# Norm factors behind the products, and a new order of the steps around the first expert gather

## The reference, cut to what matters

```python
def rmsnorm_2(x, w):                       # one factor per token, one gain per column
    y = xf * lax.rsqrt(jnp.mean(xf * xf, axis=-1, keepdims=True) + NORM_EPS)
    return (y * w.astype(jnp.float32)).astype(x.dtype)

x = x + hybrid_mixer(...)                                  # ends in mixed @ w_out
# memory_cross_attention(h = rmsnorm_2(x, norm_xa_w), ...)
q = h @ wq
scores = einsum('bshd,bmhd->bhsm', q, k) * XA_HEAD_DIM ** -0.5
p = softmax(scores);  o = einsum('bhsm,bmhd->bshd', p, v);  x = x + o @ wo
# peer_ffn(h = rmsnorm_2(x, norm_ffn_w), ...)
q = (h @ wq).reshape(t, 8, 2, 128)
sc = einsum('thpd,hpnd->thpn', q, sub_keys)                # 2 x 128 keys per head
# top 16 of each half, top 16 of their 256 sums -> 16 experts per token and head, a softmax as gate
act = gelu(u_table[expert] . h);  out = sum(gate * act * v_table[expert])
```

## Time and profile before

| | |
|---|---|
| median of three runs | 1705.7 us |
| the profiled execution | 1705.75 us, its span 1704.5 us |
| busy share of the span | PE 89%, DVE 63%, ACT 41%, POOL 21% |
| gathers by the software queue q0 | 39.4% of the 16 DMA engines' span, 277.05 MB |
| chain that ended last | PE 59%, DMA 20%, DVE 11%, ACT 5% |

### The profile page before, as it was taken

How to read it: one execution, slowest core, us unless ns; L and a number is a source line. 1 busy time by engine, 2 the same in 40 slices (tenths; PEclk the granted TensorE clock), 3 DMA queues, 4 the chain that set the end, 5 groups by cost and what they waited for, 6 DMA issues and landing times.

```text
span 1704.5 us, 21573 instructions
## 1 busy us (share of the span) xinstructions
PE 1520.0 (89%) x7972; PEld 1130.4 (66%) x7972; DVE 1073.1 (63%) x1942; ACT 701.3 (41%) x1538; POOL 349.6 (21%) x325
## 2 busy tenths in 40 slices
PE   3999989998989999798999999988888888788786
PEld 3899988888889998798998676544433443334222
DVE  6666665776555555677665128677667677677754
ACT  2434444443444444544342114444444444444443
POOL 1100010000010000101100003444444444444451
PEclk8999999899999999888999999999999999999999
DMA  9777666656455554232333438999999999999996
GB/s 359 277 240 249 236 207 222 209 199 210 173 182 185 186 185 149 87 124 87 97 112 128 177 101 342 419 420 421 420 421 420 421 421 421 421 421 422 421 419 256
DMA packets 90858, 463.14 MB, mean 272 GB/s; under 512 B 10753, under 2 KB 10913, under 8 KB 57729
## 3 DMA queue, kind: packets, MB, share of 16 engines
q0 software_dynamic: 39216, 277.05, 39.4%
q1 hardware_dynamic: 50688, 183.52, 31.9%
q10 hardware_dynamic: 848, 1.18, 0.2%
HBM read 459.62 MB, written 2.10 MB: 271 GB/s over the span
## 4 chain that ended last, share of the span: by engine, by line
PE 59%; DMA 20%; DVE 11%; ACT 5%; issue 3%; POOL 1%; SPq 0%; DVEq 0%; ACTq 0%; POOLq 0%
DMA Ft<-peer_uv,ids 14%; PE ps L1224 8%; PE ps L464 7%; PE ps L465 7%; PE ps L466 7%; DMA uhi<-peer_uv,ids 4%; PE ps L1056 3%; DVE Ft L1973 2%; PE ps L580 2%; PE ps L581 2%; PE ps L582 2%; DMA mlo<-peer_uv,ids 2%; PE ps L1139 2%; DVE wlo L1249 2%; PE ps L508 2%
## 5 line engine op out<-in xcount | busy, mean ns | idle before, releaser
L1224 PE MATMUL ps<-Ft 128*128 128x512 f32 x796 | 384.6, 621 | 76.9 <-ACT Ft L2486 76.0
L1224 PEld LDWEIGHTS ps<-Ft 128*128 128x128 f32 x796 | 146.7, 195 | 295.6 <-ACT Ft L2486 157.7
L1973 DVE CUSTOM_DVE_ANT_0 Ft<-Ft 128x1024 f32<-128x1024 f32 x199 | 243.8, 1225 | 152.3 <-DMA Ft<-peer_uv,ids 145.2
L464 PE MATMUL ps<-uhi,whi 128*128 128x256 f32 x1088 | 315.7, 290 | 7.1 <-DVE ulo L1337 6.1
L1249 DVE TENSOR_TENSOR wlo<-raw,whi 128x1024 fp32r<-128x1024 f32 x228 | 277.7, 1244 | 70.0 <-ACT whi L1997 69.6
L465 PE MATMUL ps<-ulo,whi 128*128 128x256 f32 x1088 | 311.8, 287 | 0.0
L466 PE MATMUL ps<-uhi,wlo 128*128 128x256 f32 x1088 | 311.6, 286 | 0.0
L2612 POOL DMA_INDIRECT Ft<-peer_uv,ids x199 | 220.2, 1107 | 295.3 <-PE ps L1224 258.1
L1997 ACT ACTIVATE whi<-raw 128x1024 fp32r<-128x1024 f32 x228 | 229.6, 1048 | 27.3 <-DMA raw<-ff_gu 15.6
L464 PEld LDWEIGHTS ps<-uhi,whi 128*128 128x128 f32 x1088 | 213.4, 196 | 11.2 <-issue 8.9
L465 PEld LDWEIGHTS ps<-ulo,whi 128*128 128x128 f32 x1088 | 213.0, 196 | 2.0 <-issue 0.5
(11 more groups left out here) (419 smaller groups left out, 2269.3 us busy)
## 6 DMA issues: line engine op xcount, KB each, us to landing
raw<-ff_gu SPq DMA_DIRECT2D x88, 512.0 KB, 4.8
raw<-w_ada SPq DMA_DIRECT2D x72, 512.0 KB, 5.1
raw<-ff_dn SPq DMA_DIRECT2D x44, 512.0 KB, 4.3
raw<-w_in SPq DMA_DIRECT2D x32, 512.0 KB, 3.6
raw<-w_in_s SPq DMA_DIRECT2D x28, 512.0 KB, 4.3
raw<-w_out SPq DMA_DIRECT2D x14, 512.0 KB, 4.3
raw<-w_in_m SPq DMA_DIRECT2D x12, 512.0 KB, 4.4
raw<-xa_wk SPq DMA_DIRECT2D x8, 512.0 KB, 3.6
```

The source lines that it names most:

```text
L464: t.matmul(o, hi[:, c], x[0][:, i], start=(k == 0), stop=False)
L1224: ins = t.matmul(acc[r][c], diag[n % NDIAG], gbuf[n % NGAT][:, 1024 + c * 512:1024 + (c + 1) * 512], start=False, stop=(n % 128 == 127))
L1973: v.tensor_tensor_reduce(pjunk, gbuf[n % NGAT][:, 0:1024], xn[:, q // 8, :], 1.0, 0.0, ALU.mult, ALU.add, dots[:, n:n + 1]).then_inc(*up(" ...
```

## The change

Three things are changed together.

First, the two norms of this part (cross attention's and the experts') no longer scale before the product. `columns` transposes the raw residual half by half as soon as that half is there; the gain is applied on the copy out as before. The factor per token comes later: for cross attention in the exp (its `scale` operand, and the maximum times the factor as bias), for the experts on the copy of the key scores (`choice_k`) and in `xn`. The step `row_identity` and the diagonal products go.

Second, the order on all engines. Row 0's steps come as early as their data allow. Ahead of the first expert head's keys now stand the last of the mixer's row 1, and behind them the query of head 1, row 1's transposes and all of row 1's queries, half of which stood ahead before. Row 1's softmax is cut into three steps: "soft" 0 ahead of pair 0, "soft" 1 behind pair 0, "soft" 2 behind pair 1; `values` for the two groups stand behind pairs 2 and 3.

Third, places in memory. The weight tiles get 20 places instead of 17, of which two (17 and 18) lie under the gather buffer at 12224. That buffer moves from slot 0 to slot 3, so that `first_use` is now {3: q, 5: s, 6: pT, 7: o}, all of row 1; slot 4 follows in order. GpSimd's power for row 1's first norm moves from ahead of gather 0 to behind gather 2.

```diff
-        def norm_cols(name, r):
-            t.wait_ge(*at("ms", name, r, "dgr"))
-            for b in range(2):
-                o = bank((name, "tr", r, b))
-                for k in range(4):
-                    c = (4 * b + k) * 128
-                    ins = t.matmul(o[:, k * 128:(k + 1) * 128], h[:, r, c:c + 128], dgr[:, r, :], start=True,
-                                   stop=True)
-                ins.then_inc(*up("tr", name, r, b))
-                give((name, "tr", r, b), "xTv" if b else "xTa", name, r)
+        def columns(name, src, r, b):
+
+            o = bank((name, "tr", r, b))
+            t.wait_ge(*at("res", src, b, r))
+            for k in range(4):
+                c = (4 * b + k) * 128
+                ins = t.transpose(o[:, k * 128:(k + 1) * 128], h[:, r, c:c + 128], ident)
+            ins.then_inc(*up("tr", name, r, b))
+            give((name, "tr", r, b), *taken(name, r, b))
...
             stage(0)
-            run(rows32("mixed", T_OUT, sT, ("stage_a",), 0))
+            o = rows32("mixed", T_OUT, sT, ("stage_a",), 0)
+            run(o, 6)
+            columns("xa", "mixed", 0, 0)
+            run(o, 2)
             stage(1)
             o = rows32("mixed", T_OUT, sT, ("stage_a",), 1)
-            run(o, 2)
-            norm_cols("xa", 0)
+            run(o, 1)
+            columns("xa", "mixed", 0, 1)
             run(o, 1)
             q = queries(0)
             run(q, 6)
@@ -1174,22 +1190,29 @@
             run(q, 2)
             run(o, 1)
             scores(0, 1)
-            run(o, 2)
             values_t(0, 0)
-            run(o, 2)
+            run(o, 1)
+            values(0, 0)
+            run(o, 1)
             values_t(0, 1)
-            values(0, 0)
+            w = rows32("xa", T_XO, oT, ("oTc",), 0)
+            run(w, 1)
             values(0, 1)
-            norm_cols("xa", 1)
-            run(rows32("xa", T_XO, oT, ("oTc",), 0))
+            run(w, 5)
+            columns("ffn", "xa", 0, 0)
+            run(w, 2)
+            run(o, 1)
+            columns("ffn", "xa", 0, 1)
+            run(o, 1)
+            peer_tile(0)
+            run(o, 1)
+            peer_keys(0)
+            peer_tile(1)
+            columns("xa", "mixed", 1, 0)
+            columns("xa", "mixed", 1, 1)
+            peer_keys(1)
             q = queries(1)
-            run(q, 2)
-            norm_cols("ffn", 0)
-            run(q, 1)
-            peer_tile(0)
-            run(q, 1)
-            peer_keys(0)
-            run(q, 2)
+            run(q, 6)
...
-                if what == "soft":
+                if what == "soft" and args[0] == 2:
                     for g in range(2):
                         values_t(1, g)
-                    for g in range(2):
-                        values(1, g)
+                elif what == "val":
+                    values(1, *args)
                 elif what == "out1":
                     run(out1, 1)
                 elif what == "cols1":
-                    norm_cols("ffn", 1)
+                    for b in range(2):
+                        columns("ffn", "xa", 1, b)
                 elif what == "tile":
                     peer_tile(*args)
...
-    for q in range(1, 16):
-        p = {2: 1, 3: 13, 8: 64}.get(q, 16 * q - 40)
-        first, each = {1: (0, 1), 2: (16, 1), 3: (29, 1)}.get(q, (16 * q - 24, 2))
+    for q in range(2, 16):
+        p = {2: 4, 3: 13, 8: 64}.get(q, 16 * q - 40)
+        first, each = {2: (19, 1), 3: (29, 1)}.get(q, (16 * q - 24, 2))
         for k in range(6):
             put(first + each * k, "route", q)
         put(first + 6 * each + (5 if each == 1 else 4), "drain", q)
-        if q > 1:
-            put(p, "tile", q)
-            put(p + 4, "pq", q)
...
+    for place, *what in ((0, "soft", 1), (1, "soft", 2), (2, "val", 0), (3, "val", 1), (4, "route", 1), (5, "route", 1),
+                         (6, "turn", 0), (6, "turn", 1), (10, "drain", 1), (39, "cols1"), (43, "cols1a"), (43, "mean1"),
+                         (49, "cols1v"), (100, "rows", 1), (137, "last", 0, 0), (145, "last", 0, 1),
+                         (160, "last", 0, 2)):
+        put(place, *what)
     for k in range(8):
-        put(3 + 3 * k, "out1", k)
+        put(7 + 3 * k, "out1", k)
     for n in range(2):
-        put(22 + 12 * n, "res1", n)
-        put(23 + 12 * n, "sq1", n)
-    for place, what in ((40, "mean1"), (52, "dgr1"), (53, "cols1"), (57, "cols1a"), (62, "cols1v")):
-        put(place, what)
...
-        def row_identity(name, r):
-            v.wait_ge(*at("rs", name, r))
-            v.tensor_scalar(dgr[:, r, :], ident, stat[name][:, 6 + r:7 + r], None, ALU.mult).then_inc(
-                *up("ms", name, r, "dgr"))
...
+            if g == 0:
+                v.wait_ge(*at("rs", "xa", r))
+            v.tensor_scalar(xsm[:, c:c + 2], xsm[:, c:c + 2], stat["xa"][:, 6 + r:7 + r], -1.0, ALU.mult,
+                            ALU.mult).then_inc(*up("xa_v", "m", r, g))
...
-                                   bias=xsm[:, c + e:c + e + 1], scale=1.0 / 16.0,
+                                   bias=xsm[:, c + e:c + e + 1], scale=stat["xa"][:, 6 + r:7 + r],
                                    accum_out=xsm[:, 8 + c + e:9 + c + e])
...
-            a.activation(keyed[q], spot["pk", q][:, 0:256], ACT.Copy).then_inc(*up("peer_a", "scs", q))
+            if q % 8 == 0:
+                a.wait_ge(*at("rs", "ffn", q // 8))
+            a.activation(keyed[q], spot["pk", q][:, 0:256], ACT.Copy, scale=stat["ffn"][:, 6 + q // 8:7 + q // 8]).then_inc(
+                *up("peer_a", "scs", q))
...
-        row_power("xa", 1)
         row_power("ffn", 0)
-        first_use = {4: ("q", 1, 1), 5: ("s", 1, 1), 6: ("pT", 1, 1), 7: ("o", 1, 1)}
+        first_use = {3: ("q", 1, 1), 5: ("s", 1, 1), 6: ("pT", 1, 1), 7: ("o", 1, 1)}
...
+            if n == 2:
+                row_power("xa", 1)
+            elif n == 54:
                 row_power("ffn", 1)
-            elif n == 70:
...
+    place = list(range(13)) + [18, 17, 15, 14, 16, 13, 0, 1, 2, 3, 4, 19, 5, 6, 7, 8, 9, 10, 11, 12, 13, 0, 1, 2, 3, 4, 14]
```

More of the change, by code:

```diff
@@ L192, in peer_order @@
         put(first + 6 * each + (5 if each == 1 else 4), "drain", q)
-        if q > 1:
-            put(p, "tile", q)
-            put(p + 4, "pq", q)
[L196 to L199, removed]
+        put(p, "tile", q)
+        put(p + 4, "pq", q)
+        put(p + 6, "keys", q)
+        put(p + 10, "scs", q)
+    for place, *what in ((0, "soft", 1), (1, "soft", 2), (2, "val", 0), (3, "val", 1), (4, "route", 1), (5, "route", 1),
[3 more added lines that the diff above has]
+        put(place, *what)
     for k in range(8):
-        put(3 + 3 * k, "out1", k)
+        put(7 + 3 * k, "out1", k)
     for n in range(2):
-        put(22 + 12 * n, "res1", n)
-        put(23 + 12 * n, "sq1", n)
-    for place, what in ((40, "mean1"), (52, "dgr1"), (53, "cols1"), (57, "cols1a"), (62, "cols1v")):
-        put(place, what)
[L207 to L211, removed]
+        put(25 + 12 * n, "res1", n)
+        put(26 + 12 * n, "sq1", n)
+    yield "drain", 0
+    for _ in range(4):
+        yield "route", 1
+    yield "rows", 0
+    yield "soft", 0
     for n in range(256):
@@ L217, in peer_order, with tail_places @@
         yield "last", 1, part
-def freed_by(i):
-    return i - NTAIL if i < NTAIL + NRING else i - NRING
+def tail_places():
+    place = list(range(13)) + [18, 17, 15, 14, 16, 13, 0, 1, 2, 3, 4, 19, 5, 6, 7, 8, 9, 10, 11, 12, 13, 0, 1, 2, 3, 4, 14]
+    freed, holds = [], {}
+    for i, p in enumerate(place):
+        freed.append(holds.get(p))
+        holds[p] = i
+    return place, freed
+PLACE, FREED = tail_places()
 def build(nc, D, out, known=None):
@@ L1946, in peer @@
                 elif what == "soft":
-                    for g in range(2):
-                        peak(1, g)
-                    for g in range(2):
-                        weigh(1, g)
+                    if args[0] == 0:
+                        row_mean("xa", 1, 16.0)
+                        peak(1, 0)
+                    elif args[0] == 1:
+                        peak(1, 1)
+                        weigh(1, 0)
+                    else:
+                        weigh(1, 1)
                 elif what == "turn":
@@ L2463, in peer @@
                 elif what == "soft":
-                    for g in range(2):
-                        powers(1, g)
-                    for g in range(2):
-                        weights_t(1, g)
+                    if args[0] == 0:
+                        to_q(1, 0)
+                        to_q(1, 1)
+                        powers(1, 0)
+                    elif args[0] == 1:
+                        powers(1, 1)
+                    else:
+                        for g in range(2):
+                            weights_t(1, g)
                 elif what == "sq1":
```

111 lines of the change are left out of this document (53 added, 58 removed).

## The result

The kernel after the change takes 1708.8 us (median of 12 runs, 1703.8 to 1711.3) against 1703.3 us for the kernel before (12 runs, 1698.6 to 1706.6). The ratio is 1.0033 with a 95% interval from 1.0018 to 1.0048: slower by 5.6 us, 3.1 to 8.2. The forecast was +5.3. The absolute number, 1711.0, is 2.2 too high, since it started from 1705.7 and twelve runs put the kernel before at 1703.3. One execution of the version with softmax and values whole took 3009.6 us, against 1691 to 1701 for its other nine, and is left out of its ratio.

The account below looks back on a forecast made before the run. The full DMA engines bound the kernel; gather 7 at 1055.4 instead of gather 0 at 1031.1, less 17.9 and 2.5, gave +3.9, and one clock dip of 1.4 made +5.3: 1711.0 us from 1705.7, range 1702 to 1717.

Parts of the forecast that it names:

- Gather 0 sooner by 11.2 us: TensorE ahead of the first keys: 11.7 us of work and stall removed, less 0.5 for a late weight tile.
- Row 1's queries done at +95.8: TensorE after the keys: queries end at 1033.3 instead of 1029.7, with a 2.4 us wait for head 1's second tile.
- Scale operands for nothing: Scale on exp and key copy, factor in the maximum: between 0 and 0.1 us each, taken as 0.
- Diagonal 1 at +106.1: ScalarE's chain of exps, three table loads and pairs 0 and 1's diagonals, ending at 1043.6 in trace time.
- Gathers 6 and 7 at +108.9 and +117.9, one clock dip on top: Gathers 6 and 7 issued at 1046.4 and 1055.4 behind row 1's softmax and values; one TensorE dip adds 1.4 us.
- The sum: Change of the end: gather 7 at 1055.4 less gather 0's 1031.1, less 17.9 for seven gathers and 2.5 for weights, +3.9.
- Equal time with gather 7 at 1051.5: Break-even: with gather 7 issued at 1051.5 the change would take as long as the kernel before.
- The rule on table loads: ScalarE's three table loads: a drain of 1.38 us more each, sum 4.1 us higher, +9.4; rival at 1715, chance 0.03.
- gather 0 decides: Rival: buffers 3 to 7 free early enough, so the end moves with gather 0; 1692 to 1702, chance 0.12.
- No change at all: Rival: no change worth measuring, gather 7 between 1048 and 1054.9, time near 1707; chance 0.22.
- The long dip: Rival: TensorE at half clock through pairs 0 to 3 and both values, gather 7 at 1060 to 1063, 1715 to 1719; chance 0.12.
- That gather 0 might not come earlier: Rival: TensorE waits for weights elsewhere, so all later releases slip too; 1718 or more, chance 0.02.

Follow-up runs that it names:

- split version: The kernel before with only row 1's softmax and values cut up among pairs 0 to 3 as in the change: 1.0075 of before, +12.8 us.
- held gather: The change with gather 0 held on GpSimd until row 1's first four query tiles are done: 1.0026 of the kernel before, +4.4 us.
- first four experiments: In order of telling: the change with softmax and values whole (0.9948), the same with xn behind (0.9952), before with softmax split (1.0075), the change without gelu (0.9992).
- fast version with the hold: The change with row 1's softmax and values whole ahead of pair 0, xn behind them, and gather 0 held back: 0.9958 of before, -7.2 us.
- version with late values: The change with row 1's softmax whole ahead of pair 0, its values still behind pairs 2 and 3: 1.0009 of before, +1.5 us.
- the one with all in one piece: The change with row 1's softmax and values whole and ahead of pair 0: 0.9948 of the kernel before, -8.9 us.
- three fast orders: The change with softmax and values whole (0.9948 of before), the same with xn behind them (0.9952), and that with gather 0 held as well (0.9958).

## Why the prediction was right, point by point

Its times are turned here into times from the first mixer product, by 937.5. (Read from the start of the trace, gather 7 came at 1055.50 where 1055.4 was forecast; but this execution reached the part 1.6 us earlier, so that is partly luck.)

- **Gather 0 sooner by 11.2 us.** 11.9. The stall of 0.5 that I charged for head 0's second tile did not come: TensorE's row shows no idle time ahead of it. (The last row is the end of row 1's queries, for the next point.)

```profile
1001.32 1.95 PE L1152 MATMUL ps<-ulo,Ft 128*128 128x128 f32 x16
1003.10 1.95 PE L1152 MATMUL ps<-ulo,raw 128*128 128x128 f32 x16
...
1006.61 0.61 PE L1165 MATMUL ps<-Ft 128*128 128x128 f32 x4
1007.05 1.95 PE L1152 MATMUL ps<-ulo,whi 128*128 128x128 f32 x16
1010.40 2.05 PE L1152 MATMUL ps<-ulo,whi 128*128 128x128 f32 x16 [1.40 <-DMA whi<-peer_wq]
...
1026.81 3.73 PE L1099 MATMUL ps<-uhi,Ft 128*128 128x128 f32 x32
```

- **Row 1's queries done at +95.8, behind a wait of 2.4 us.** +94.7, behind a wait of 1.40 (the two last rows above). The place was right, the size 1 us too large. They stood at +92.2 before, so they are later though gather 0 is sooner, which is what the forecast rested on.
- **Scale operands for nothing.** Nearly. The exp of 128x256 takes 0.56 us with the factor as its scale (L2403) and 0.47 without (L2382 in before and in its split version). Four of them are 0.4 us on ScalarE's chain: the size was off, by little.
- **Diagonal 1 at +106.1.** It ended at 1041.36 + 0.40 = +105.9. The microsecond that the queries had won went into the longer exps and the handovers.
- **Gathers 6 and 7 at +108.9 and +117.9, one clock dip on top.** +110.8 and +119.6. They are 1.9 and 1.7 us later than forecast, and that is the dip, which I had put at 1.4: pair 1 took 1.7 us more at half clock. That it came at all is in part luck. The forecast drew it from TensorE's waits, and the size it took from row 1's values; but the split version of before has the same waits (1.94 and 2.62 us) and no dip. Without it the same sum would have said +3.9. The gap from gather 6 to 7 is 8.9 us, forecast 9.0.
- **Breaks of 3 us and 6 us in the data.** The windows show both. By their shares the DMA engines lose 10 us between 1041 and 1058.
- **The sum.** With the measured gather times it gives 119.64 - 93.59 - 17.9 - 2.5 = +5.6, and the trace has +4.8. The two query tiles at 2.5 are borne out: 655.9 less 653.5 is 2.4. The 0.8 left over lies on before's side of the sum. The split version of before, whose end hangs on gather 7 as well, misses in the same way: 123.60 - 93.59 - 17.9 is +12.1 against before, and its trace has +11.2. What it is was not tested; I would put it to before's own start: between 1035 and 1040 its trace has a DMA share of 0.99 but only 374 GB/s, where 421 is full, so its first gathers were not worth the full 2.55 us each.
- **Equal time with gather 7 at 1051.5.** From the constant for the change, before's end would need gather 7 at 768.3 - 653.5 = +114.8, which is 1052.3 in before's own times. The version without gelu had it at +114.5 and ended at +768.0, beside before's +768.3.
- **The rule on table loads.** By the drain that the Trainium skill (ScalarE: Activation LUTs, "What ACT_TABLE_LOAD costs") adds to each switch, about 1.38 us, the change would have cost 4 us more; that is an estimate from the page's figure. The three loads above take 1.29, 1.29 and 1.30 us from their start to that of the next instruction, and the second starts 0.02 us after the end of the diagonal ahead of it. The traces do not agree with that drain.

So the mechanism held, and that the number fits to 0.3 us in the runs and 0.5 us in the trace is also because a dip 0.3 larger than forecast and the 0.8 on before's side stand against each other.

Of the rivals, "gather 0 decides" fell with the held gather. No change at all is outside the interval (3.1 to 8.2 us); the upper edge of that rival, +3.4, is just inside it, and what speaks against it is gather 7, which came at 1057.1 in before's times where the rival needed it before 1054.9. The long dip did not come, since the clock is 1.00 again from 1046; its times had a slip besides, as gather 7 at 1060 to 1063 makes 1714 to 1717 by the sum, not 1715 to 1719. That gather 0 might not come earlier was answered by +81.7.

The range and the side held. What was wrong is the level: three runs of before were 2.4 us above the later median, and the spread of 8 us between executions arises ahead of the part, which I had not looked for. Its cause was not tested, but it goes with the granted clock. Of the 22 runs of before beside the first four experiments, the nine with a mean clock of 0.963 or 0.964 took 1703.7 to 1706.6 us, and the four at 0.968 or 0.969 took 1698.7 to 1700.5 us. Between the traces of before (937.49) and of the fast version with the hold (929.60) the granted clock in 400 to 500 us is 0.93 and 0.96.

## What to carry to other kernels

Where a stretch at the end is bound by DMA, its time is set by the last transfer that was late, not by the first that is early: take the issue of the last one behind which the engines stay full, and add the bytes that are left. In these traces a wait in the in-order DMA queue was free while the issued data covered it, and cost about its full length from there on (in the split version of before, gather 7 14.4 us later, the end 11.2), so ahead of moving work behind the first transfers, ask which buffer's release it carries. And count from a fixed instruction at the start of the changed part: from there gather 0 came at +93.6 in all three kernels in before's order, within 0.01 us, where whole executions of one kernel differ by 8 us. Single traces, so counted, gave differences within 2.6 us of those of the runs, and inside their intervals but for before without gelu, where they gave +0.6 and the interval ends at +0.2.

## What the runs showed that was not expected

- The end lies 653.46, 653.47, 653.47 and 653.57 us behind gather 7 in four kernels whose beginnings differ by 6 us. 249 gathers in a full stretch are that regular.
- The waits do not tell whether the clock falls. TensorE fell to half clock behind waits of 2.0 and 2.8 us in the change, and so it did with gather 0 held (pair 1 in 3.36 us, the transposes in 1.39). It did not in the version without gelu, whose waits there are 0.6 and 0.8. But the split version of before, with 1.94 and 2.62, kept 1.00; and behind a wait of 2.48 us ahead of the transposes the clock fell in the version with late values and not in the one with all in one piece. What decides it is open. In the three fast orders the clock stayed at 1.00 from 1025 to 1070.
- A DMA share of 0.99 does not say that the bytes flow: from 1035 to 1040 it goes with 374 GB/s in before (the first gathers) and with 346 in the change (gathers 3 to 5), where 421 is reached later at 1.01. The cause is open.
